# Low parts of the last two gate panel loads on GpSimd, latent queries ahead of the retention's products, two gate units behind the last turn

## The reference

```python
for l in range(DEPTH):                         # DEPTH = 2
    p = rms_norm(h, attn_norm[l]) @ w_in[l]
    rq, rk, rv, rg, pw, qa, kva, gl = split(p)
    y_ret  = retention_mix(rq, rk, rv, rg)     # 4 heads of 128, decayed scores
    y_rwkv = rwkv7_mix(pw, ...)                # 8 heads of 64, state over chunks of 64 tokens
    y_mla  = mla_mix(qa, kva, ...)             # 8 heads, queries and keys from normed latents
    gates  = sigmoid(gl)                       # three gates of 1024 columns
    h += (sum_n gates[n] * (y[n] @ w_branch[l, n])) @ w_o[l]
    h += swiglu(...) if l == 0 else top_2_of_8_experts(...)
out = rms_norm(h, final_norm)
```

## Time and profile before

| | us |
|---|---|
| median of 3 runs (lowest, highest) | 1901.74 (1898.72, 1906.24) |
| the profiled execution's own time | 1901.2 |
| its span, first to last instruction | 1899.2 |
| TensorE busy in the span | 1862.2 (98%) |
| VectorE busy | 1442.9 (76%) |
| ScalarE busy | 1162.0 (61%) |
| GpSimd busy | 170.3 (9%) |
| mean granted clock of TensorE | 0.994 |

### The profile page before, as it was taken

One profiled execution on the slowest core, in us unless ns is written; L12 is line 12 of the kernel. 1 busy time (PEld: TensorE's weight loads), 2 busy tenths in 40 slices (PEclk: granted clock), 3 DMA queues, 4 the chain that ended last, 5 costly groups with the idle time before them and its releaser, 6 DMA issues.

```text
span 1899.2 us, 26635 instructions
## 1 busy us (share of the span) xinstructions
PE 1862.2 (98%) x10282; PEld 1508.3 (79%) x10282; DVE 1442.9 (76%) x1487; ACT 1162.0 (61%) x1149; POOL 170.3 (9%) x164
## 2 busy tenths in 40 slices
PE   8999999999999999999999999999999999999998
PEld 7868776788888687667888888888888888888886
DVE  5688575644556686764998989988888899898897
ACT  5565323443444663244777777777777777777776
POOL 1353005000002540040000000000000000000000
PEclk9999999999999999998999999999999999999999
DMA  9642224654566332224999999999999999999995
GB/s 329 197 155 96 90 90 152 209 180 144 188 208 202 129 133 90 90 90 152 361 365 341 368 345 359 367 346 357 362 348 365 348 354 363 343 365 347 359 366 222
DMA packets 182542, 487.79 MB, mean 257 GB/s; under 512 B 5897, under 2 KB 12677, under 8 KB 173641
## 3 DMA queue, kind: packets, MB, share of 16 engines
q1 hardware_dynamic: 177296, 477.50, 69.6%
q0 software_dynamic: 1488, 5.57, 0.8%
q10 hardware_dynamic: 3688, 3.74, 0.7%
HBM read 482.03 MB, written 1.05 MB: 254 GB/s over the span
## 4 chain that ended last, share of the span: by engine, by line
PE 91%; DVE 5%; ACT 2%; issue 1%; DMA 0%; DVEq 0%; SPq 0%; ACTq 0%
PE bank L1845 48%; PE bank L1247 27%; PE bank L1460 2%; PE bank L1239 2%; PE bank L1794 2%; PE bank L1431 1%; PE bank L1856 1%; PE bank L1814 1%; DVE y_rwkv L1913 1%; DMA ring<-w_in_dram 0%; DVE xterm L1913 0%; DVE xc L2250 0%; PE bank L1383 0%; PE bank L1493 0%; PE bank L1338 0%
## 5 line engine op out<-in xcount | busy, mean ns | idle before, releaser
L1913 DVE TENSOR_TENSOR w_lo<-ring,w_hi 128x2048 fp32r<-128x2048 f32 x337 | 767.1, 2289 | 112.6 <-ACT w_hi L1149 104.8
L1149 ACT ACTIVATE w_hi<-ring 128x2048 fp32r<-128x2048 f32 x320 | 612.2, 1916 | 122.8 <-PE bank L1845 112.2
L1845 PE MATMUL bank<-w_hi,xg_hi 128*128 128x512 f32 x896 | 354.4, 396 | 1.1 <-DVE w_lo L1913 1.1
L1845 PE MATMUL bank<-w_hi,xg_lo 128*128 128x512 f32 x896 | 349.7, 390 | 0.0
L1845 PE MATMUL bank<-w_lo,xg_hi 128*128 128x512 f32 x896 | 349.5, 390 | 0.0
L1845 PEld LDWEIGHTS bank<-w_hi,xg_hi 128*128 128x128 f32 x896 | 168.8, 188 | 38.0 <-DVE w_lo L1913 4.1
L1845 PEld LDWEIGHTS bank<-w_hi,xg_lo 128*128 128x128 f32 x896 | 168.2, 188 | 35.5
L1845 PEld LDWEIGHTS bank<-w_lo,xg_hi 128*128 128x128 f32 x896 | 168.4, 188 | 33.9 <-issue 0.2
L1845 PE MATMUL bank<-w_hi,ehT_hi 128*128 128x512 f32 x448 | 176.5, 394 | 0.0
L1845 PE MATMUL bank<-w_hi,ehT_lo 128*128 128x512 f32 x448 | 174.8, 390 | 0.0
L1845 PE MATMUL bank<-w_lo,ehT_hi 128*128 128x512 f32 x448 | 174.5, 390 | 0.0
(11 more groups left out here) (434 smaller groups left out, 3028.6 us busy)
## 6 DMA issues: line engine op xcount, KB each, us to landing
ring<-moe_w_gate_dram SPq DMA_DIRECT2D x57, 2048.0 KB, 7.8
ring<-moe_w_up_dram SPq DMA_DIRECT2D x56, 2048.0 KB, 8.1
ring<-moe_w_down_dram SPq DMA_DIRECT2D x56, 2048.0 KB, 9.6
ring<-w_in_dram SPq DMA_DIRECT2D x26, 2048.0 KB, 8.5
ring<-w_branch_dram SPq DMA_DIRECT2D x6, 2048.0 KB, 8.2
ring<-ffn_w_gate_dram SPq DMA_DIRECT2D x5, 2048.0 KB, 8.2
ring<-ffn_w_up_dram SPq DMA_DIRECT2D x5, 2048.0 KB, 8.0
ring<-ffn_w_down_dram SPq DMA_DIRECT2D x5, 2048.0 KB, 8.4
```

What stands on the lines that cost most here:

```text
L1149: A.activation(w_hi[:, q % PARTS, :], ring[:, i, o:o + HALF], ACT.Copy).then_inc(s.hi_ready, 1)
L1845: ins = M(dst, a, w, start=start and n == 0, stop=stop and n == 2, skip_group_check=True)
L1913: return V.tensor_tensor(out_, a, b, op)
```

## The change

In both layers:

- GpSimd makes the low parts of quarters 16 to 23 (gate panels 4 and 5) between its last high part and its `k_lo` work; VectorE's eight `g_low` calls go. TensorE waits for a new semaphore for these quarters.
- The latents are turned before the retention's scores, and the latent queries `mq` are made before the retention's outputs `oR`. ScalarE copies the latents before the two sigmoids of RWKV (L897, L899) and the queries before `oR`. VectorE masks the scores before it scales the decays (L2093).
- The load of branch 0 is waited for (`branch_slot(0)`) after the first pair products, not before them.
- Of the last four gate units only 92 and 94 stay ahead of the last branch; 93 and 95 follow the turn of RWKV's last rows. `gt11` thereby moves behind `yT11` in the list. `last_branch(0, 1)` goes ahead of `turn_merged(0)`. VectorE gates both parts of the first tile's last branch, makes `turned_low(1)`, and then adds. ScalarE takes `gate(11)` behind `turned_tile(1)` and `k_high(4)` behind `merged_out(0)`.

Once: SyncE issues the load of the first weight panel before that of the second half of `x`; the routing has 9 idle products in place of 6 ahead of the ranks, and 5 new ones behind them.

```diff
     out += [(f"rT{s}{t}", A) for t in range(T) for s in range(2)]
+    out += [(f"cT{t}", A) for t in range(T)]
     out += [(f"sR{h}", V) for h in range(RH)]
-    out += [(f"cT{t}", A) for t in range(T)]
+    out += [(f"mq{t}{u}", A) for t in range(T) for u in range(2)]
     out += [(f"oR{t}", A) for t in range(T)]
-    out += [(f"mq{t}{u}", A) for t in range(T) for u in range(2)]
...
-    out += [("gt10", A), ("gt11", A), ("br100", V), ("br110", V), ("yT11", V), ("gT00", A), ("gT01", A)]
-    out += [("br101", V), ("br111", V), ("o00", V), ("gT10", A), ("gT11", A)]
+    out += [("gt10", A), ("br100", V), ("br110", V), ("yT11", V), ("gt11", A), ("br101", V), ("gT00", A), ("gT01", A)]
+    out += [("br111", V), ("o00", V), ("gT10", A), ("gT11", A)]
...
@@ block.sync
-        for t in range(T):
-            sp.dma_start(h[:, t, :], x[0, t * P:(t + 1) * P, :]).then_inc(x_loaded[t], 16)
+        sp.dma_start(h[:, 0, :], x[0, 0:P, :]).then_inc(x_loaded[0], 16)
         for n, (kind, l, j, _) in enumerate(PANELS):
             if n == 1:
+                sp.dma_start(h[:, 1, :], x[0, P:2 * P, :]).then_inc(x_loaded[1], 16)
                 for t in range(T):
                     sp.wait_ge(x_loaded[t], 16)
...
@@ block.gpsimd
+            for n in range(16, QUARTERS):
+                pool.wait_ge(s.act_g_hi_ready, 12 * l + n - 11)
+                G.tensor_tensor(g_quarter(l, n, ring_lo), g_quarter(l, n), g_hi[G_PLACE[n]][:].bitcast(F32),
+                                ALU.subtract).then_inc(s.pool_g_lo_ready, 1)
             for n in range(8):
                 pool.wait_ge(s.k_hi_ready, 8 * l + n + 1)
...
@@ block.scalar, end of the mixer
             gate(10)
-            gate(11)
             gn_root(2, 8)
             turned_tile(1)
-            k_high(4)
+            gate(11)
             merged_out(0)
-            for n in range(5, 8):
+            for n in range(4, 8):
                 k_high(n)
...
@@ block.tensor
+            pe.wait_ge(s.qa_ready, l + 1)
+            for t in range(T):
+                b = bank(f"cT{t}.{l}")
...
             read_out(pe, f"rT11.{l}")
             for i in range(RH):
                 b = bank(f"sR{i}.{l}")
...
+            read_out(pe, f"cT1.{l}")
+            for t in range(T):
+                for u in range(2):
+                    project(f"mq{t}{u}.{l}", cT, slot, 2, 384, t, 384 * u, 768)
             read_out(pe, f"sR3.{l}")
...
                 if t == 0:
                     branch_in(0)
-                    ret_slot = branch_slot(0)
...
+                if t == 0:
+                    ret_slot = branch_slot(0)
                 branch(0, ret_slot, t, t)
...
-            gate_units(92, 96)
+            gate_units(92, 93)
+            gate_units(94, 95)
             branch_slot(1)
...
             transpose_tile(f"yT11.{l}", y_rwkv, 1, 0, 4)
+            gate_units(93, 94)
+            gate_units(95, 96)
+            last_branch(0, 1)
             turn_merged(0)
-            last_branch(0, 1)
             last_branch(1, 1)
...
-        keep_on(b, 6)
+        keep_on(b, 9)
...
+        keep_on(banks[BANK_OF["router.1"]], 5)
...
@@ block.vector, end of the mixer
-            merge(0, 0)
-            merge(1, 0)
+            parts = [gated(1, u, 0) for u in range(2)]
             turned_low(1)
+            settle()
+            for u in range(2):
+                step(tt(merged[:, 0, 512 * u:512 * u + 512], sigs[0][:, u, 0, :], parts[u], ALU.add), s.merged_done)
             merge(0, 1)
```

More of the change, by code:

```diff
@@ L297, in __init__ @@
         self.g_lo_ready = new("g_lo_ready")
+        self.pool_g_lo_ready = new("pool_g_lo_ready")
         self.g_used = new("g_used")
@@ L895, in _ @@
                     copy_out(f"rT{q}{t}.{l}", qkT[:, q, :, t, :])
[L896 to L899, removed]
             if l == 0:
@@ L908, in _ @@
                     own.step(ins) if i < 2 else own.free(ins, f"cT{t}.{l}")
+            read_out(act, f"z1.{l}")
+            own.step(A.activation(ld[:], ld[:], ACT.Sigmoid), s.decay_sig_ready)
+            read_out(act, f"a1.{l}")
+            own.step(A.activation(ab[:], ab[:], ACT.Sigmoid), s.rate_sig_ready)
             def g_high(n):
@@ L919, in _ @@
             for t in range(T):
-                copy_out(f"oR{t}.{l}", y_ret[:, t, :])
+                for u in range(2):
+                    copy_out(f"mq{t}{u}.{l}", mq[:, t, 4 * u:4 * u + 4, :], 384)
             g_high(0)
             for t in range(T):
-                for u in range(2):
-                    copy_out(f"mq{t}{u}.{l}", mq[:, t, 4 * u:4 * u + 4, :], 384)
+                copy_out(f"oR{t}.{l}", y_ret[:, t, :])
             for t in range(T):
@@ L1306, in _ @@
                     done(ins)
+            pe.wait_ge(s.qa_ready, l + 1)
+            for t in range(T):
+                b = bank(f"cT{t}.{l}")
+                for i in range(2):
+                    TR(b[:, i * P:(i + 1) * P], qa[:, t, i:256:2], ident)
+                done(TR(b[:, 256:384], qa[:, t, 256:384], ident))
             read_out(pe, f"rT11.{l}")
@@ L1313, in _ @@
             slot = panel("mla")
-            pe.wait_ge(s.qa_ready, l + 1)
+            read_out(pe, f"cT1.{l}")
             for t in range(T):
[L1316 to L1319, removed]
+                for u in range(2):
+                    project(f"mq{t}{u}.{l}", cT, slot, 2, 384, t, 384 * u, 768)
             read_out(pe, f"sR3.{l}")
@@ L1331, in _ @@
                 done(ins)
[L1332 to L1335, removed]
             for t in range(T):
@@ L1362, in gate_units @@
                     if r == 0:
-                        pe.wait_ge(s.g_lo_ready, QUARTERS * l + n + 1)
+                        if n < 16:
+                            pe.wait_ge(s.g_lo_ready, 16 * l + n + 1)
+                        else:
+                            pe.wait_ge(s.pool_g_lo_ready, 8 * l + n - 15)
                     x = 2 * (n % 4) + c
@@ L2082, in g_low @@
             def g_low(n):
-                if n < 4 or n > 15:
-                    dve.wait_ge(s.act_g_hi_ready, 12 * l + (n if n < 4 else n - 12) + 1)
+                if n < 4:
+                    dve.wait_ge(s.act_g_hi_ready, 12 * l + n + 1)
                 else:
@@ L2091, in _ @@
             settle()
-            dve.wait_ge(s.decay_sig_ready, l + 1)
-            step(V.tensor_scalar(ld[:], ld[:], -DECAY, None, ALU.mult), s.logd_ready)
             for i in range(RH):
@@ L2098, in _ @@
                      f"sR{i}.{l}")
+            dve.wait_ge(s.decay_sig_ready, l + 1)
+            step(V.tensor_scalar(ld[:], ld[:], -DECAY, None, ALU.mult), s.logd_ready)
             dve.wait_ge(s.rate_sig_ready, l + 1)
@@ L2219, in _ @@
                 if t:
-                    g_low(19)
                     tile_variance(0)
@@ L2259, in _ @@
                     step(add_gated(2, 1, 0))
-                else:
-                    g_low(16)
                 for lv in range(LEVELS):
@@ L2276, in _ @@
                 if t:
-                    g_low(20)
                     step(add_gated(2, 0, 1))
-                    g_low(21)
                     turned_low(0)
                 else:
-                    g_low(17)
                     gated(0, 0, 1)
@@ L2295, in _ @@
                         step(add_gated(2, 0, 0))
-                    if n > 1:
-                        g_low(20 + n)
                     if n == 3:
@@ L2310, in _ @@
                     if n == 0:
-                        g_low(18)
                         gated(0, 1, 0)
```

## The result

The changed kernel took 1910.79 us (median of 12, 1907.25 to 1914.48), the kernel before 1902.05 beside it (12 runs, 1898.72 to 1906.93). The ratio is 1.0047, with a 95% interval from 1.0038 to 1.0056: slower by 0.47%, which by the bound of 0.5% set ahead still counts as within, though narrowly: the interval reaches beyond that bound. The forecast was 1908.1. The profiled execution took 1907.25 (span 1905.4); it is the shortest of the twelve.

The account below looks back on a forecast made before the run. TensorE, busy 1862.2 of 1899.2 us, was taken as the bound. Start +1.0, latents -3.8, chain with pair products +5.3, mixer ends +2.1 and +3.8, routing -1.5 made +6.9 on 1901.2: 1908.1 us, range 1894 to 1915.

Parts of the forecast that it names:

- Low parts on GpSimd: the chain: Tile 0, each layer: GpSimd's low parts of quarters 16 and 17 stall VectorE's serial chain; +2.65 a layer, +5.3 in both.
- first rival: VectorE's short chain operations slip past GpSimd unheld; the sum loses 5.8, giving 1902.3 us; chance 0.20.
- Tile 1: VectorE's chain is free there; quarters 19 and 22 fall beside a scaling of the state, costed at nothing.
- End of the mixer: Last gate units to output_halves(0): late second o panel and held VectorE work; +2.1 in layer 0, +3.8 in layer 1.
- Latents: Latents ahead of the retention's scores: waits of 0.84 and 1.71 go, new wait of 0.6; 1.9 won a layer, -3.8.
- Pair products: Pair products ahead of the branch load: of the 1.44 wait only 0.25 is won each layer, VectorE's own work deciding.
- Start: First panel ahead of x's second half: panel 0 earlier, panel 1 later; +1.0, bounds 0.5 won to 2.3 lost.
- Routing: Eight more idle products may bring the clock back before the gathering; -1.5, bounds -3.4 to +0.9.
- third rival: Pauses in each layer bring falls of the clock; with four of eight, 1914.5 us; chance 0.22.
- second rival: Holes close as ordered: panel o 1 does not decide, GpSimd leaves VectorE alone; -8.9, 1892.3 us; chance 0.18.

Follow-up runs that it names:

- the two back on VectorE: Changed kernel with the low parts of gate quarters 16 and 17 back on VectorE at their old places: 1905.69 us, ratio 1.0020.
- low-part-later run: Kernel before with latents and routing changed, plus VectorE making quarter 15's low part behind the last mixer's first gated product: 1896.15 us, ratio 0.9971.
- new start alone: Kernel before with only the new order of transfers at the start (first panel ahead of the second half of x): 1904.77 us, ratio 1.0020.
- old-start run: Changed kernel with the old order of transfers put back (both halves of x ahead of panel 0): 1910.71 us, ratio 1.0049.

## Why the prediction was right, step by step

**Low parts on GpSimd: the chain.** Right in mechanism and near in size: forecast were +2.65 a layer, the trace has a wait of 2.36 in both and the two back on VectorE returned 5.1 by the medians. Counted from the gate units behind the new wait, TensorE starts the identity products 2.3 later in layer 0 and only 1.2 in layer 1, where the wait of 0.81 for `sig` is gone. The first rival (short operations slip past) is out: one of 56 columns was held for 2.21 us. The single-input reductions between them took their 0.2. Here "SBUF — State Buffer" of the Trainium skill, section "Who interferes with whom", is borne out: it makes the lock one of ports and of issue order, and lets the shape of an operation play no part. It also says that `tensor_scalar` can enter a mode that takes the shared ports; the 128 x 8 one that took 1.26 us beside GpSimd and 0.32 without agrees.

**Tile 1.** I cost quarters 19 and 22 at nothing. One scaling of the state was held beside each (128x256, 2.11 and 2.22 for 0.43), and TensorE did not feel it: 83.7 us from the identity products to the state's last ones, 84.0 before.

**End of the mixer.** The late panel was forecast at 8.2 us behind its request and took 8.4. The stage came out 0.8 shorter in both layers than forecast (28.9 from the end of the state's products, not 29.7), so +1.4 and +3.0 in place of +2.1 and +3.8. The term that was too large is VectorE's two low parts of the merged rows: 4.00 in both layers, not 4.7, so that TensorE waited 0.96 and 0.81 for them and not 1.8. VectorE's delay was put on the subtraction of the mean; the instruction ahead of it was held, for 0.94 and not 1.4.

**Latents.** 2.5 a layer were forecast for the first gate unit, 2.65 and 2.67 came; behind the new wait for quarter 1, which came at 0.22 for 0.6, 2.1 and 2.2 are left, where 1.9 were forecast.

**Pair products.** I said that the 1.44 would win only 0.25, since VectorE's own work decides there. By the trace it won nothing, for the wait is still there. The small size was about right, the reason incomplete: a second wait of the same length lay under the first. From the 17th pair product on TensorE needs the bank of the last head, VectorE frees it behind the low part of quarter 15, and that stands 4.09 us for GpSimd's high part. The low-part-later run removed one lock and won nothing, the change removed the other and won nothing, and both together won 1.0 a layer by the trace.

**Start.** The term that was mis-sized most: +1.0 with bounds to 2.3, where the first retention turn came 4.0 later (116.25 to 120.25) and the new start alone cost 3.3 by the medians. I had the request of panel 1 some 3 us later and its landing at most 2.5, with a slack of 0.9 to take off; the request came 4.5 later and ScalarE's start 3.0. What the term missed: the queues were nearly empty for 3 us while everything up to panel 2 waits for transfers, which made panel 1's first product 2.2 late, at the upper bound, and a second fall of the clock (1.7) stands behind the pause, for which the term had nothing.

**Routing.** −1.5 forecast, −2.4 in this trace, by the mechanism named. The eight products are 16 instructions of 0.12 at full clock, 1.9 us of work, and the waits of 0.61 and 0.70 that stood there took in 1.3 of it; the gain hangs on how many falls there are (10.2 us at 0.50 there before, 3.4 after), and these differ between executions.

**Sum and rivals.** Start +4.0, latents −4.3, from there to the state's last products +4.6 in both layers together (the two waits of 2.36 and layer 1's fall of the clock, 1.7, less what came back), ends +1.4 and +3.0, routing −2.4: that makes +6.3, with the span's +6.2 beside it and +6.9 forecast. That these two are so close is in part luck: the start was put 3.0 too low, and the other four terms were too high by 3.6 together (latents 0.5, chain 0.7, ends 1.5, routing 0.9). The median moved by 8.7. The 2.5 between them is the third rival in small: over the twelve runs the mean clock is 0.9928, against 0.9941 in the kernel before (the experiments' runs of it), and 0.995 in the one profiled. The second rival is out: panel o 1 does decide (waits of 1.89 and 1.98 for it, and 28.9 us for the stage where that rival had 24.7).

## What to carry to other kernels

Price work on GpSimd by what stands on VectorE beside it, not by its own time: two operations of 2.4 us that nobody waits for held two links of a serial chain with two SBUF operands by 2.0 and 2.2 us, though such a link alone takes 0.2. Before a wait is removed, take it as gone and ask for the next condition of this instruction and of those right behind it; here the two ended within 0.6 us of each other and had to go together. In a stage that lives on transfers, count the bytes not moved while a queue waits, not the slack of the first consumer.

## What the runs showed of the hardware that was not expected

TensorE's fall from 2.4 to 1.2 GHz came in pieces: nearly every one in the fourteen profiled executions, but for the last microseconds of the span, is a stretch of 3.4 us at 0.50, or two to four in a row, each worth 1.7 us. Many stand behind a pause of 1.9 to 5.0 us, yet the same pause has one in some executions and none in others: the pause of 2.36 in layer 0 had one in the old-start run and none in the changed kernel. For the runs of the kernel before in the three series, a mean granted clock of 0.993 goes with 1903.6 us (10 runs) and 0.995 with 1900.6 (14 runs): 3.0 us for 0.2%, somewhat less than the 3.8 that 0.2% of the span is. Differences of 3 us between single executions are the clock's until shown otherwise.
